# Hybrid backbone step on one core: the RWKV state scan through chunk transition matrices, with the side steps in blocks

## What is computed

```
def step(s, inp):
    rt, wt, kt, vt, at, bt = inp
    sa = jnp.einsum('bhij,bhj->bhi', s, at)
    s = s * wt[:, :, None, :] + sa[..., None] * bt[:, :, None, :] + vt[..., None] * kt[:, :, None, :]
    return s, jnp.einsum('bhij,bhj->bhi', s, rt)
```

## Time and profile before

| | |
|---|---|
| time, median of 3 runs | 2222.88 us |
| profiled execution | 2218.59 us, span 2216.8 us |
| PE busy | 1940.5 us (88%) |
| DVE busy | 1051.9 us (47%) |
| ACT busy | 837.6 us (38%) |
| POOL busy | 283.4 us (13%) |
| HBM read | 209.10 MB, 96 GB/s over the span |

### The profile page before, as it was taken

One profiled execution on the slowest core, in us unless ns is written; L12 is line 12 of the kernel. 1 busy time (PEld: TensorE's weight loads), 2 busy tenths in 40 slices (PEclk: granted clock), 3 DMA queues, 4 the chain that ended last, 5 costly groups with the idle time before them and its releaser, 6 DMA issues.

```text
span 2216.8 us, 32378 instructions
## 1 busy us (share of the span) xinstructions
PE 1940.5 (88%) x13395; PEld 1550.2 (70%) x13395; DVE 1051.9 (47%) x1931; ACT 837.6 (38%) x1408; POOL 283.4 (13%) x550
## 2 busy tenths in 40 slices
PE   6899998967995798999989989898687569899998
PEld 2799445634554598999979965465445458799998
DVE  0335426754566554443342544384566646443332
ACT  1533534253333445333253345324324334533321
POOL 2000000014555000000000000000544420000000
PEclk9999999988996799999999999999887569999999
DMA  7433333202130143443433433333101003344442
GB/s 257 133 117 105 101 114 124 96 24 77 58 115 20 35 151 95 120 128 104 131 104 118 125 99 114 101 100 100 58 3 56 2 1 119 95 115 133 113 117 84
DMA packets 267769, 214.07 MB, mean 97 GB/s; under 512 B 7209, under 2 KB 259400, under 8 KB 267368
## 3 DMA queue, kind: packets, MB, share of 16 engines
q1 hardware_dynamic: 264640, 204.39, 30.3%
q0 software_dynamic: 2736, 7.54, 1.1%
q10 hardware_dynamic: 248, 0.07, 0.0%
HBM read 209.10 MB, written 2.88 MB: 96 GB/s over the span
## 4 chain that ended last, share of the span: by engine, by line
PE 67%; DVE 11%; ACT 8%; POOL 7%; issue 4%; PEld 1%; DMA 1%; PEldq 1%; ACTq 0%; DVEq 0%; POOLq 0%
PE bank L547 11%; PE bank L549 11%; PE bank L548 10%; PE bank L598 7%; PE bank L603 6%; POOL cst L1128 4%; POOL lora L1126 3%; PE bank L1047 3%; PE bank L1045 3%; PE bank L1046 3%; PE bank L609 2%; PE bank L787 2%; PE bank L499 1%; ACT h L1192 1%; DVE scr_rounded L1600 1%
## 5 line engine op out<-in xcount | busy, mean ns | idle before, releaser
L549 PE MATMUL bank<-scr_rounded 128*128 128x384 f32 (+1 forms) x1312 | 442.8, 337 | 0.0
L547 PE MATMUL bank<-scr_rounded 128*128 128x384 f32 x672 | 231.5, 345 | 36.0 <-DVE scr_rounded L1605 34.2
L549 PEld LDWEIGHTS bank<-scr_rounded 128*128 128x128 f32 (+1 forms) x1312 | 248.6, 189 | 1.0
L603 PE MATMUL bank<-h,ring 128*128 128x384 f32 x640 | 236.8, 516 | 3.9 <-DMA ring<-in_w_in_dram 2.1
L548 PE MATMUL bank<-scr_rounded 128*128 128x384 f32 x672 | 229.3, 341 | 0.0
L547 PE MATMUL bank<-scr_rounded,gate_rounded 128*128 128x384 f32 (+1 forms) x640 | 214.0, 334 | 4.4 <-DVE scr_rounded L1600 4.4
L1600 DVE TENSOR_TENSOR scr_rounded<-ring,scr_rounded 128x2048 fp32r<-128x2048 f32 (+1 forms) x64 | 136.0, 2126 | 167.7 <-ACT scr_rounded L1183 166.8
L548 PE MATMUL bank<-scr_rounded,gate_rounded 128*128 128x384 f32 (+1 forms) x640 | 213.8, 334 | 0.0
L598 PE MATMUL bank<-ring,scond 128*2 128x256 f32 x768 | 179.9, 387 | 20.0 <-DVE mg L1590 6.0
L603 PEld LDWEIGHTS bank<-h,ring 128*128 128x128 f32 x640 | 120.9, 198 | 92.9 <-issue 23.5
L1600 DVE TENSOR_TENSOR scr_rounded<-ring,gate_rounded 128x2048 fp32r<-128x2048 f32 (+3 forms) x64 | 130.1, 2033 | 104.2 <-ACT gate_rounded L1183 103.7
(11 more groups left out here) (357 smaller groups left out, 3250.6 us busy)
## 6 DMA issues: line engine op xcount, KB each, us to landing
ring<-in_w_in_dram SPq DMA_DIRECT2D x56, 1024.0 KB, 5.3
ring<-in_w_ada_dram SPq DMA_DIRECT2D x48, 1024.0 KB, 5.4
ring<-in_w_ffn_in_dram SPq DMA_DIRECT2D x88, 512.0 KB, 5.1
ring<-in_w_ffn_out_dram SPq DMA_DIRECT2D x32, 704.0 KB, 4.6
ring<-in_w_out_dram SPq DMA_DIRECT2D x8, 1024.0 KB, 5.2
ring<-in_w_po_a_dram SPq DMA_DIRECT2D x4, 1024.0 KB, 6.4
ring<-in_w_po_b_dram SPq DMA_DIRECT2D x4, 1024.0 KB, 5.3
ring<-in_w_po_c_dram SPq DMA_DIRECT2D x4, 1024.0 KB, 5.2
```

The costliest lines, as they stand in the source:

```text
L547: pe.matmul(o, w_hi[:, k, :], right[0][k], start=k == 0, stop=False)
L549: ins = pe.matmul(o, w_lo[:, k, :], right[0][k], start=False, stop=k == nk - 1)
L603: ins = pe.matmul(b[:, 0:T], w[:, k, 128 * (j % 2):128 * (j % 2) + 128], h[:, k, :], start=k == 0, stop=k == KD - 1)
```

## The change

For each pair n, three 64x64 matrices are formed per chunk and direction ahead of the scan, for all six chunks at once: `FT` (the transition of the state, plus the identity `eye`), `GG` (what the chunk adds to the state) and `RT` (how the outputs read the state). With them a scan step is one product H for each direction and one DVE instruction. R and U are gone. Seven sets of 12 products for each direction are new: AT, RV (in `turned`), WZ, VZ, FT, GG (in `transitions`) and RT (in `reads`).

The order changes too. `grams(n + 1)` now closes the block of n, and DVE starts POOL on n + 1 inside `inverses(n)`, straight behind the two transposes out of `W`. A block n is: `inverses`/`merges`, `transitions`, three scan steps and `outputs`, all for n - 1, then `factors(n)`, `turned(n)`, `grams(n + 1)`. The side steps stand in `fill(FILLS[n][...])` around `factors`. One `fill(1)` stays in `merges`; none is left in the scan. Gates, bonus and head means of the end move ahead of the last scan.

```diff
+        FILLS = ((2, 10, 4, 0), (4, 4, 6, 0), (4, 4, 6, 0), (2, 2, 0, 6))
...
+                def chunkwise(kind, key, n, d, left, right):
+                    pe.wait_ge(*room())
+                    b = item(key, kind, l, n, d)
+                    for c in range(6):
+                        for h in range(2):
+                            ins = pe.matmul(b[hr[h], 64 * c:64 * c + 64], left(h, c), right(h, c), start=True, stop=True)
+                    ins.then_inc(psum_ready, 1)
+
+                def transitions(n):
+                    pe.wait_ge(*emptied("G2", l, n))
+                    for d in range(2):
+                        pe.wait_ge(*emptied("AT", l, n, d))
+                        chunkwise("WZ", "V", n, d, lambda h, c: ZZ[hr[h], d, c, :], lambda h, c: AT[hr[h], d, c, :])
...
                 def scan_step(n, s):
                     for d in range(2):
...
-                        b = item("V", "R", l, n, s, d)
-                        for x, c in enumerate(scanned(d, s)):
-                            for h in range(2):
-                                rows = hr[1 - h] if s == 0 and x == 0 else slice(0, 128)
-                                ins = pe.matmul(b[hr[h], 64 * x:64 * x + 64], MMt[rows, d, h, c, 0:64], Q[rows, d, h, c, :], start=True, stop=True)
-                        ins.then_inc(psum_ready, 1)
-                    fill(1)
...
-                    fill(1)
...
                         b = item("V", "H", l, n, s, d)
-                        for x, c in enumerate(scanned(d, s)):
+                        for x, c in enumerate([scanned(d, s)[-1]] + ([scanned(d, 1)[0]] if s == 0 else [])):
                             for h in range(2):
-                                ins = pe.matmul(b[hr[h], 64 * x:64 * x + 64], BK[:, d, h, c, :], Q[:, d, h, c, :], start=True, stop=True)
+                                ins = pe.matmul(b[hr[h], 64 * x:64 * x + 64], FT[hr[h], d, c, :], state(d, c)[hr[h]], start=True, stop=True)
                         ins.then_inc(psum_ready, 1)
-                    fill(1)
...
+                loras(2)
+                grams(0)
                 for n in range(5):
...
                     if n:
-                        for s in range(4):
-                            scan_step(n - 1, s)
+                        merges(n - 1)
+                        transitions(n - 1)
+                        scan_step(n - 1, 0)
+                        reads(n - 1)
+                        scan_step(n - 1, 1)
+                        scan_step(n - 1, 2)
                         outputs(n - 1)
                     if n < 4:
+                        fill(FILLS[n][0])
                         factors(n)
-                        fill((14, 2, 2, 2)[n])
-                        merges(n)
                         if n < 3:
                             loras(2 * n + 3)
+                        fill(FILLS[n][1])
+                        turned(n)
+                        fill(FILLS[n][2])
+                        if n < 3:
+                            grams(n + 1)
+                            if n < 2:
+                                loras(2 * n + 4)
+                    if n == 3:
+                        for hp in range(4):
+                            gated(hp)
+                        for hp in range(4):
+                            bonus(hp)
+                        for hp in range(3):
+                            head_mean(hp)
                         fill(2)
+                        for hp in range(3):
+                            head_var(hp)
+                        fill(FILLS[n][3])
...
                 def inverses(n):
                     dve.wait_ge(S["rw_inv"], told("rw_inv", l, n + 1))
                     dve.transpose(Zbn.rearrange("p u j -> p j u"), W).then_inc(*step())
                     dve.transpose(ZbT.rearrange("p u i -> p i u"), W.rearrange("p j i -> p i j")).then_inc(*step())
                     dve.wait_ge(*last())
+                    if n < 3:
+                        begin(n + 1)
```

More of the change, by code:

```diff
@@ L1006, in _ @@
-                for hp in range(4):
-                    pe.wait_ge(S["rw_ysq"], told("rw_ysq", l, hp + 1))
-                    pe.wait_ge(*room())
-                    b = item("A", "gnv", l, hp)
-                    pe.matmul(b[:, 0:T], blocks, gate[:, hp, :], start=True, stop=True).then_inc(psum_ready, 1)
-                pe.wait_ge(*emptied("H", l, 3, 2, 1))
+                        fill(FILLS[n][1])
[5 more added lines that the diff above has]
+                                loras(2 * n + 4)
@@ L1017, in _ @@
                     ins.then_inc(psum_ready, 1)
+                head_mean(3)
+                head_var(3)
                 finish(l, 3)
@@ L1478, in _, with gates, head_scales @@
                 exps(1)
+                def gates(hp):
+                    side_work("gc", l, hp)
+                    act.wait_ge(psum_ready, filled("gc", l, hp))
+                    b = bank("gc", l, hp)
+                    A(kkb[hp], b[:, 0:T], ACT.Copy).then_inc(*empties("gc", l, hp))
+                def head_scales(hps):
+                    for hp in hps:
+                        act.wait_ge(*emptied("gnm", l, hp))
+                        A(sq[hp], pc[:, hp, :], ACT.Square).then_inc(*tells("rw_ysq"))
+                    for hp in hps:
+                        side_work("gnv", l, hp)
+                        act.wait_ge(psum_ready, filled("gnv", l, hp))
+                        b = bank("gnv", l, hp)
+                        A(sq[hp], b[:, 0:T], ACT.Ln, bias=eps[:, 2:3], scale=1.0 / HD).then_inc(*empties("gnv", l, hp))
+                    act.wait_ge(*last())
+                    for hp in hps:
+                        A(sq[hp], sq[hp], ACT.Exp, scale=-0.5).then_inc(*tells("rw_yr"))
                 for n in range(5):
@@ L1482, in _ @@
                     if n:
[L1483 to L1484 removed]
+                        merges(n - 1)
+                        transitions(n - 1)
                     if n < 3:
                         exps(2 * n + 2)
+                    if n:
+                        outputs(n - 1)
                     if n < 4:
[L1488 to L1491 removed]
                         factors(n)
[L1493 removed]
                         if n < 3:
@@ L2005, in _ @@
                 cp(h0.rearrange("p a b -> p (a b)"), b[:, 0:512]).then_inc(*empties("s0T", l))
+                grams(0)
+                begin(0)
                 for n in range(5):
-                    if n < 4:
-                        grams(n)
-                    if n == 0:
-                        logs(2)
-                    else:
-                        for s in range(4):
-                            scan_step(n - 1, s)
-                            if s == 0 and n < 3:
-                                logs(2 * n + 2)
-                        side_work("Y", l, n - 1)
-                        dve.wait_ge(psum_ready, filled("Y", l, n - 1))
-                        b = bank("Y", l, n - 1)
-                        cp(pc[:, r_ + n - 1, :], b[:, 0:T]).then_inc(*empties("Y", l, n - 1))
+                    if n:
+                        inverses(n - 1)
+                    if n < 3:
+                        logs(2 * n + 2)
+                    if n:
+                        transitions(n - 1)
+                        scan_step(n - 1, 0)
+                        reads(n - 1)
+                        scan_step(n - 1, 1)
+                        scan_step(n - 1, 2)
                     if n < 4:
                         factors(n)
-                        inverses(n)
                         if n < 3:
```

348 lines of the change are left out of this document (179 added, 169 removed).

## The result

| | before | after |
|---|---|---|
| median | 2222.44 us (4 runs, 2217.31 to 2224.97) | 2198.86 us (4 runs, 2196.63 to 2199.02) |
| ratio after/before, 95% interval | | 0.9894 [0.9876, 0.9913] |
| span of the profiled execution | 2216.8 us | 2197.1 us |
| PE busy | 1940.5 us | 1946.5 us |
| mean granted clock of PE | 0.924 | 0.952 |

The kernel became 1.06% faster. I had forecast 2233 us, slower: the time lies inside the range, and the sign was wrong.

The account below looks back on a forecast made before the run. The RWKV phases were taken as a chain of handoffs with PE its longest part. Layer 0 losing 16 us and layer 1 gaining 6 gave +10 on 2218.6; with 4.3 for the median, 2233, range 2193 to 2262.

Parts of the forecast that it names:

- `transitions` 9.2, bounds 6.9 to 11.6: Eight sets of 24 records in each chain: 6.9 us at full clock, 11.6 at low, 9.2 taken.
- Low clock through the first half of `transitions`: PE was to run the first half of that row at low clock, giving 9.2 us instead of 6.9.
- Reads, H, outputs 8.5: Behind `transitions`: last drain, H, RT sets and two H 5.6 us, outputs 2.9 at full clock.
- `merges` 6.6 and 7.2: G1, the remaining side step, G2 and ACT's copies at the chain's start: 6.6 us, with an ada side step 7.2.
- Idle 6.3 before `merges`: Between `grams` and `merges` PE idles 6.3 us in each block while DVE does 7.8 us of work.
- Side products held by ACT: Behind `factors` PE waits for ACT to drain a bank: 4.3 us, 6.4 and 5.7 named, each with 1.7 of low clock.
- Layer 0 loses, layer 1 gains: Over the two RWKV phases, layer 0 was to lose 16 us and layer 1 to gain 6.
- Factors, side steps, `grams`: PE's work around `factors`: `factors` 6.8 us, AT and RV 3.5, `grams` 1.8, side steps 1.34 or 1.82 each.
- full cover: Transitions at full clock (18 us less) and shorter side-product waits (17 less) give 2198; chance 0.33.
- rival two: POOL's substitutions decide the block length; each layer loses 60 us and more, 2130 or less; chance 0.05.
- rival three: Clock stays low through transitions, reads, H and outputs: 5.9 us more per chain, about six hit, +35, 2268; chance 0.15.

Follow-up runs that it names:

- e5: The kernel after with each product of WZ, VZ, FT and GG issued twice, 1536 records more; ratio to before 1.0090, +44 us against after.
- e1: The kernel after with POOL's start on the next n moved behind the product into `ZZ`; ratio to before 0.9877, -4 us against after.
- e3: The kernel after with another FILLS table, so no third side product in a row stands behind `factors`; ratio to before 0.9805, -20 us against after.
- e7: The kernel after with extra products ahead of `merges`, and two more between G1 and G2 in three chains; ratio to before 0.9839, -12 us against after.
- e2: The kernel after with DVE's start of POOL on the next n put off until the last scan step; ratio to before 1.0080, +41 us against after.
- e6: The kernel after with 20 more POOL products of 128x240 behind the substitutions of n = 1 and 2; ratio to before 0.9931, +8 us against after.
- e4: The kernel after with extra PE products in the wait for DVE ahead of `merges`; ratio to before 0.9859, -8 us against after.
- f5_all: The kernel after with another FILLS table, side steps inside the chain, POOL's start behind `ZZ`, and extra PE products; ratio to before 0.9721, -38 us against after.

## Why the prediction was wrong

The step that failed is the price of the chain from the end of `merges` to the end of the outputs. I priced it at 17.7 us in each block (9.2 for `transitions`, 5.6 for H, RT, H, H, and 2.9 for the outputs). The eight measured 13.6, 15.2, 13.6, 14.9 in layer 0 and 13.6, 16.3, 15.1, 15.8 in layer 1: 118 us in sum against 142. These 24 us are most of the 30 by which the profiled execution missed (+10 forecast, -20 measured). They are three terms: the price of a set at the high clock, 0.86 us against a measured 0.75 (7 us over the 64 sets); the low clock in `transitions`, put at 2.3 us above the high-clock price in each chain and measured at 1.2 on the mean (9 us); and H, the RT sets and two H, 5.6 against 4.7 (7 us). The outputs' 2.9 was right.

- *`transitions` 9.2, bounds 6.9 to 11.6.* Measured 6.0 to 8.7, and 6.0 in three chains, so the lower bound itself was broken. Nothing in the earlier trace rows gives 0.86: a set by itself takes 0.92, and the two sets at 586.62 take 1.55 from start to start, 0.78 each. In the row of four, 96 records take 3.02 us, 0.75 a set. e5 gives nearly the same price by time: 29 ns a record, 0.69 a set.
- *Low clock through the first half of `transitions`.* So in two of the eight; three had the high clock before the row began, and three got it inside the first 96 records. I had given all eight one value for what changes with a microsecond of start, as e1 shows.
- *Reads, H, outputs 8.5.* Measured 7.6.
- *`merges` 6.6 and 7.2.* Right (6.6 to 7.0) but for n = 3: 5.1 against 7.6 in layer 0, where not ACT's variance chain but the table load and drain of a side product held the copy, for 1 us, and 4.9 against 6.2 in layer 1.
- *Idle 6.3 before `merges`.* Right: 6.33, 6.28, 6.32, 6.28; 7.8 and 8.2 at n = 2, 3.5 at n = 3 of layer 1.
- *Side products held by ACT.* Right in sum (20.7 forecast, 6.41 + 4.63 + 6.44 + 5.22 = 22.7 measured), wrong in the split; e3 shows that they are on the path.
- *Layer 0 loses, layer 1 gains.* Right in order, 15 us too high in each: +16 and -6 against +1 and -21.
- *Factors, side steps, `grams`.* Right within 1 us where laid out, but AT and RV took 2.8 to 3.1 against 3.5 in seven of the eight blocks, by the same price of a set; `terms` of layer 1 bound PE for 3 us less (12.1 against 15.2), and the held side products again cost 3 us of low clock in blocks 0, where I had 1.7.

Of the rivals, full cover named this time, 2198, and that is in part luck. It has two terms: the cheaper `transitions` (18 us) came true in size (16), nearly half of it through a price of a set that the rival did not have; the shorter waits of side products (17 us) did not come true, and other terms made up for them. The substitutions did not decide in this kernel (rival two), and the low clock through the whole first row happened in two chains of eight, in none of them through reads, H and outputs (rival three). The chance of 0.33 for full cover was too low: the rows gave a price at the high clock for every part of the chain, and the 9.2 between the two bounds was a guess.

What stays open: why the clock came back before the row in some blocks and within it in others, and why the row of n = 3 in layer 0 stays slow in e7, and how the gain splits between the new scan and the new order.

## What to carry to other kernels

Replacing a chain of short dependent products by a dense row of more products can be cheaper than its record count says: here 13.6 to 16.3 us at a granted clock of 0.82 to 1.00, against 20.9 and 21.9 at 0.51 and 0.69 for the bare chain of handoffs. Price such a row from the densest rows of the same form in the trace, and carry the clock as a range for each block, not one guess for all. Look at what queue a side product's drain stands in before putting three in a row, and keep POOL's long stretches away from DVE's work on operands in SBUF.

## What the runs showed of the hardware

- DVE beside POOL: a TENSOR_TENSOR of 128x384 with both operands in SBUF took 0.55 us alone and 0.94 with POOL's TENSOR_TENSORs beside it; with one operand in PSUM all 64 of L2047 took 0.55 to 0.56 us in after, and the same 64 did in e2 and e6, some of them beside POOL's widest products (timelines of DVE). By the Trainium skill, "GPSIMD Engine Reference" (Specifications), POOL shares its SBUF interfaces with VectorE and contends with instructions that have two SBUF inputs. The trace agrees, with the number of 1.7 times. It also shows more: a TENSOR_SCALAR of 128x384 took 0.47 us alone and 0.77 and 0.59 in e2, and POOL's own products of 128x240 there took 0.62 and 0.65 us ahead of 579 and 0.80 to 0.89 behind, beside DVE's `terms`.
- fp32 records of 64x64 in a dense row, alternating between two 64x64 corners of PE: 31 ns at the high clock, 56 ns at the low. By the Trainium skill, "TensorE: Matmul & The Clock Gate" (Back-to-back issue gap), up to 64 columns cost some 60 cycles, 25 ns at full clock, as the gap of an isolated product; in a stream with a weight load for each product the spacing is set by both. The trace has 31 with one weight load for each record (360 and 360 in the window at 549.60), so the measured value is to be used.
- Behind the waits of 6.3 us ahead of `merges` the granted clock was at its level of 1.2 GHz each time (G1 1.49 us), and at 2.4 GHz each time in e4, where extra products filled them (0.95). Behind waits of 3.5 us both were seen (1.49 after, 0.95 in e1), and behind waits of 2.6 us too (0.95 in e4, 1.49 in f5_all, both at n = 2 of layer 0). In e1, where the work of n = 0 in layer 0 began 1.1 us earlier, its first row took 2.4 us more.
